# Layer 0's shift and scale summed by TensorE as columns, in a two-layer attention block on one core

## The chip, the core and the metric

The kernel runs on one core of a Trainium2 chip. The metric is the device time of one execution in microseconds (us). In the profile, PE is TensorE's matmuls, PEld its weight loads, DVE is VectorE, ACT is ScalarE, POOL is GpSimd and SP is SyncE, from whose queue the weights are loaded.

## The reference

Two layers, each with three kinds of attention in parallel (latent, windowed, axial), over 512 image tokens (x) and 256 context tokens (ctx) of width 1024. What matters here is how a layer begins: its input is normed, scaled and shifted by two vectors that are products of the conditioning rows with a 1024x3072 matrix.

```
def hybrid_layer(x, ctx, c, c_ctx, lw, pos, update_ctx):
    mod_x = jax.nn.silu(c) @ lw['ada_w'] + lw['ada_b']
    mod_c = jax.nn.silu(c_ctx) @ lw['ada_w'] + lw['ada_b']
    shift, scale, gate = jnp.split(mod_x[:, None, :], 3, axis=-1)
    c_shift, c_scale, c_gate = jnp.split(mod_c, 3, axis=-1)
    h = rmsnorm(x, lw['norm_w']) * (1 + scale) + shift
    hc = rmsnorm(ctx, lw['norm_w']) * (1 + c_scale) + c_shift
    p = h @ lw['w_in']
    ...
```

In layer 0 nothing can be projected before shift and scale are there.

## The kernel before

`schedule()` writes one list of events; `build()` then runs over that list once for each engine and issues what belongs to it, so the order of the list is the order on every engine. Tokens stand in six tiles of 128 (TT = 6): context tiles 0 and 1, image tiles 2 to 5. `first_modulation()` writes the start of layer 0, up to the first projections.

The first two thirds of `ada_w` (shift, then scale) are loaded as 16 chunks of 128 rows x 1024 columns, 512 KB each, into 16 buffers of their own (`FIRST`); D is 1024, KD is 8 and P is 128. The names w_raw_134 to w_raw_141 are the eight buffers of the shift third and w_raw_142 to w_raw_149 those of the scale third. `cs_n` holds silu of the two conditioning rows (x and ctx) as columns, 128x2 for each row chunk.

- The shift third is summed by VectorE. Event `AD` adds chunk times column for both rows of conditioning, into the PSUM tiles `wide` and `ptp`. Its last step writes into w_raw_140 and w_raw_141, and TensorE then sums over the partitions with `ones` as the moving operand, in a group of kind `adc` (lines 1394 and 2022).
- The scale third is summed by TensorE. Event `AF` (line 1414) holds `cs_n` (128x4, two columns of it zero) stationary and streams 512 columns of the chunk, twice per chunk. In the first five chunks a third matmul (line 1419) goes to `acc[1]`, where nobody reads it. ScalarE copies the two 4x512 sums to `a_row` (event `AC`, lines 1745 and 1746), and TensorE turns them into columns (event `AT`, line 1424).
- Event `MOD` (lines 2135 and 2141) adds the bias to the scale and forms `mod_a`; the shift is in `mod_col`.

A token tile goes through four events. `XQ`: ScalarE sums its squares and takes the root (lines 1789 and 1793). `XN`: the row is multiplied by its inverse root, into one of two buffers `xn`, by VectorE (line 2160) or by ScalarE (line 1801). `XT`: TensorE turns it, eight 128x128 transposes into `wide` or `ptp` (line 1497). `XM`: ScalarE and VectorE each scale and shift one half into one of two buffers `x_mod` (lines 1815 and 2180), ScalarE copies to `h_hi` (lines 1819 and 1822), GpSimd subtracts for `h_lo` (line 1912). Event `W` splits a weight chunk into `w_hi` (ScalarE, line 1632) and `w_lo` (GpSimd, line 1850). The projections' matmuls are at line 1394: w_raw_52 and w_raw_55 hold the two `early` chunks.

In the list, image tiles a and b (2 and 3) are normed and turned before `MOD`; c and d, and then the two context tiles, follow it. When context tile 1 is through, ScalarE squares the first projection (line 1648), VectorE reads it (lines 1969 and 1970), and TensorE goes on at 61.66 us with the next ones.

Of the kernel before, what the change touches and what calls it, by code (L numbers as in the profile page):

```python
# [5 lines left out]
D = 1024  # L6
# [3 lines left out]
P = 128  # L10
KD = D // P
# [115 lines left out]
def schedule():  # L127
# [414 lines left out]
    used, side_shift = {}, [0]  # L542

    def first_modulation():

        shift_row, shift_sums = row_sums(0, 0, FIRST[:KD])
        sums, scale = [], []
        for third in (0, 0, 0, 1, 0, 0, 1, 0, 1, 0, 1, 0, 1, 1, 1, 1):
            if third == 0:
                sums.append(shift_row(len(sums)))  # L550
            else:
                scale.append(chunk("adr", 0, 1, len(scale), (0, 1), slot=FIRST[KD + len(scale)]))
                whole.add(scale[-1])
                used[scale[-1]] = 0
        early = chunk("win", 0, C_AK, P), chunk("win", 0, C_CKV, P)
        a, b, c, d = x_first(0)[:4]
        holding[0] = True
        for k in range(KD):
            run_all(sums[k])
            emit("AF", c=scale[k], k=k)  # L560
            if k == 2:
                emit("VT")
            if k == KD - 3:
                emit("VC")
            if k == KD - 2:
                for tt in (a, b):
                    square_rows(0, tt, 0)
        for tt in (a, b):
            norm_rows(tt, by="v")
        emit("AC")  # L570
        run_all(shift_sums((0,)))
        turn_rows(a)
        emit("AT")
        turn_rows(b)
        emit("W", c=early[0])
        for tt in (c, d):
            square_rows(0, tt, 0)
        emit("W", c=early[1])
        n["split"] = early[1] + 1
        norm_rows(c)  # L580
# [11 lines left out]
        read_other()  # L592
        side_shift[0] = n["free"]
        for tt in x_first(0)[4:]:
            square_rows(0, tt, 0)
        norm_rows(x_first(0)[4])
        modulate_rows(d)
        holding[0] = False
# [30 lines left out]
    def norm_rows(tt, by="a"):  # L629
        emit("XN", tt=tt, n=row_of[tt], by=by)  # L630
# [4 lines left out]
    def modulate_rows(tt):  # L635
        emit("XM", tt=tt, n=row_of.pop(tt), mod=n["mod"], shift=side_shift[0] if tt < TT_CTX else 0)
# [285 lines left out]
def build(nc, t_in, out):  # L922
# [33 lines left out]
    cs_n = fixed("cs_n", [P, KD, 4], F)  # L956
# [46 lines left out]
    a_row = shared("a_row", [4, D], F, 83968)  # L1003
# [32 lines left out]
    with ExitStack() as stack:  # L1036
# [17 lines left out]
        af_done, at_done = semaphore("af_done"), semaphore("at_done")  # L1054
        row_copied = semaphore("row_copied")
# [106 lines left out]
        def _(sp):  # L1162
            new = counting()
            for c in range(len(chunks)):
# [74 lines left out]
        def first_sums(half):  # L1239
            return pv[0:4, :] if half == 0 else wide[0:4, D:D + 512]  # L1240
# [87 lines left out]
        def _(pe):  # L1328
# [5 lines left out]
            for e in events:  # L1334
# [72 lines left out]
                elif ev == "AF":  # L1407
                    c, k = e["c"], e["k"]
# [11 lines left out]
                elif ev == "AT":  # L1420
# [820 lines left out]
```

## Time and profile before

| | us |
|---|---|
| median of 3 runs | 1752.57 (1751.98 to 1753.06) |
| the profiled execution | 1752.6 |
| its span in the profile | 1750.8 |
| TensorE matmuls busy | 1673.6 (96%) |
| VectorE busy | 1022.5 (58%) |
| ScalarE busy | 1063.0 (61%) |
| GpSimd busy | 624.6 (36%) |
| mean granted TensorE clock | 0.991 of full |

Times in the trace count from the start of the span. A row of a timeline is one instruction or several alike in a row: its start, its length, what it is, how many records of it (x16), and in brackets how long the engine sat idle before it and for what. A float32 matmul that is no transpose leaves two records. PEclk is the clock that TensorE was granted, as a share of 2.4 GHz.

### The profile page before, as it was taken

The page shows a single profiled execution, that of the slowest core. Times are in us where ns is not written, and L with a number is a line of the kernel's source. Part 1 is how long each engine was busy: PE and PEld are TensorE (multiplying, and loading weights), DVE is VectorE, ACT ScalarE, POOL GpSimd, SP SyncE. Part 2 cuts the span into 40 slices and gives each one's busy share as a digit, 9 for nine tenths or more (in the row PEclk, how much of TensorE's full clock was granted, in tenths as well). Part 3 has the DMA queues.
Part 4 walks back from the last instruction along what each step waited for, and adds up shares of the span by engine and source line. Part 5 has one row for each costly group of instructions (what it writes and reads, how often), then busy time and mean ns, then how long its engine had stood idle before and what let it go on. Part 6 is the DMA issues. An engine that isn't in the chain of part 4 may idle for free.

```text
span 1750.8 us, 26994 instructions
## 1 busy us (share of the span) xinstructions
PE 1673.6 (96%) x10400; PEld 1465.8 (84%) x10400; DVE 1022.5 (58%) x2116; ACT 1063.0 (61%) x1967; POOL 624.6 (36%) x426
## 2 busy tenths in 40 slices
PE   6999999999999999999999999999999998999997
PEld 2778888889988889999889987888888887888787
DVE  6345766665556655545773535566676666555633
ACT  4545777776666767765321264678777678777322
POOL 1533333333333323322322254443344433333442
PEclk9999999999999999999999999999999999999999
DMA  8111111111111112011734322111122221212642
GB/s 321 52 37 29 26 46 37 49 31 49 49 55 49 33 41 55 25 44 47 234 115 171 119 76 73 41 38 46 49 55 67 73 73 33 70 51 53 204 146 95
DMA packets 178531, 129.51 MB, mean 74 GB/s; under 512 B 21658, under 2 KB 167652, under 8 KB 178404
## 3 DMA queue, kind: packets, MB, share of 16 engines
q1 hardware_dynamic: 174240, 115.36, 23.0%
q10 hardware_dynamic: 2884, 8.24, 1.3%
q0 software_dynamic: 1280, 4.20, 0.7%
q8 instruction: 82, 1.34, 0.3%
q14 instruction: 45, 0.37, 0.1%
HBM read 123.58 MB, written 4.19 MB: 73 GB/s over the span
## 4 chain that ended last, share of the span: by engine, by line
PE 74%; DVE 11%; ACT 10%; issue 3%; DMA 1%; POOL 0%; SPq 0%; DVEq 0%; ACTq 0%
PE acc L1394 54%; PE wide L1447 6%; PE ptp L1465 6%; PE pv L1478 4%; PE pv L1479 3%; DVE nmax L2067 2%; ACT e L1715 2%; DVE pt L2092 1%; ACT w_hi L1632 1%; DVE q_s L1584 1%; DVE k_m L1584 1%; DVE k_s L1584 1%; ACT k_m L1575 1%; ACT x_mod L1815 1%; DMA w_raw<-in_ada_w 1%
## 5 line engine op out<-in xcount | busy, mean ns | idle before, releaser
L1850 POOL TENSOR_TENSOR w_lo<-w_raw,w_hi 128x1024 fp32r<-128x1024 f32 (+2 forms) x192 | 391.0, 2039 | 562.8 <-ACT w_hi L1632 561.0
L1394 PE MATMUL acc<-h_hi,w_hi 128*128 128x512 f32 (+2 forms) x1320 | 464.7, 353 | 11.8 <-DVE lf L1970 4.7
L1394 PE MATMUL acc<-h_hi,w_lo 128*128 128x512 f32 (+2 forms) x1320 | 461.6, 351 | 0.0
L1394 PE MATMUL acc<-h_lo,w_hi 128*128 128x512 f32 (+2 forms) x1320 | 458.1, 351 | 0.6 <-POOL h_lo L1912 0.6
L1394 PEld LDWEIGHTS acc<-h_hi,w_hi 128*128 128x128 f32 (+1 forms) x1320 | 249.0, 189 | 50.5 <-issue 12.2
L1730 ACT ACTIVATE pt<-ptp 128x512 fp32r<-128x512 f32 (+3 forms) x312 | 165.5, 563 | 194.6 <-PE ptp L1465 192.7
L1394 PEld LDWEIGHTS acc<-h_hi,w_lo 128*128 128x128 f32 (+1 forms) x1320 | 248.9, 189 | 34.0
L1394 PEld LDWEIGHTS acc<-h_lo,w_hi 128*128 128x128 f32 (+1 forms) x1320 | 246.1, 188 | 34.9 <-POOL h_lo L1912 1.0
L2067 DVE TENSOR_REDUCE nmax<-wide 128x1 f32<-128x768 f32 (+3 forms) x240 | 190.1, 792 | 107.7 <-PE wide L1447 104.4
L1904 POOL TENSOR_TENSOR o_t<-o_half,o_t 64x256 f32<-64x256 f32 x120 | 91.4, 762 | 434.5 <-DVE o_half L2099 432.3
L1722 ACT ACTIVATE e<-e,einv 128x768 f32<-128x768 f32 (+3 forms) x240 | 193.4, 806 | 60.2 <-DVE einv L2084 59.7
L2092 DVE TENSOR_TENSOR pt<-ptp,pt 128x512 fp32r<-128x512 f32 (+3 forms) x312 | 192.0, 641 | 45.9 <-ACT pt L1730 45.8
L1632 ACT ACTIVATE w_hi<-w_raw 128x1024 fp32r<-128x1024 f32 (+2 forms) x192 | 172.8, 903 | 57.1 <-DMA w_raw<-in_w_out 53.9
L1465 PE MATMUL ptp<-ident,e 128*128 128x128 f32 x1152 | 161.4, 273 | 0.6 <-ACT e L1722 0.5
L1715 ACT ACTIVATE e<-wide,nbias,rq 128x768 f32<-128x768 f32 x160 | 144.9, 906 | 19.6 <-DVE nbias L2073 16.3
L1465 PEld LDWEIGHTS ptp<-ident,e 128*128 128x128 f32 x1152 | 131.1, 140 | 3.2 <-ACT e L1722 0.9
L1447 PE MATMUL wide<-k_s,q_s 128*128 128x256 f32 (+2 forms) x576 | 124.8, 334 | 0.0
L1478 PE MATMUL pv<-pt,v_s 128*128 128x256 f32 (+1 forms) x384 | 99.1, 285 | 13.2 <-DVE pt L2092 10.3
L1394 PE MATMUL acc<-og_hi,w_hi 128*128 128x512 f32 (+1 forms) x288 | 102.9, 357 | 0.0
L1394 PE MATMUL acc<-og_lo,w_hi 128*128 128x512 f32 (+1 forms) x288 | 102.7, 357 | 0.0
L1394 PE MATMUL acc<-og_hi,w_lo 128*128 128x512 f32 (+1 forms) x288 | 102.6, 356 | 0.0
L1479 PE MATMUL pv<-pt,v_s 128*128 128x256 f32 (+1 forms) x384 | 97.6, 282 | 0.0
(217 smaller groups left out, 3064.3 us busy)
## 6 DMA issues: line engine op xcount, KB each, us to landing
w_raw<-in_w_in SPq DMA_DIRECT2D x102, 512.0 KB, 3.9
w_raw<-in_ada_w SPq DMA_DIRECT2D x48, 512.0 KB, 5.5
w_raw<-in_w_out SPq DMA_DIRECT2D x16, 512.0 KB, 3.5
w_raw<-in_w_in SPq DMA_DIRECT2D x16, 256.0 KB, 3.1
w_raw<-in_w_o_mla SPq DMA_DIRECT2D x16, 256.0 KB, 2.8
w_raw<-in_w_o_swa SPq DMA_DIRECT2D x16, 256.0 KB, 2.8
w_raw<-in_w_o_ax SPq DMA_DIRECT2D x16, 256.0 KB, 2.8
w_raw<-in_mla_w_uq SPq DMA_DIRECT2D x16, 144.0 KB, 2.4
```

What stands on the lines that cost most here:

```text
L1394: ins = nc.tensor.matmul(dst, lhs, rhs, start=first, stop=last)
L1447: ins = nc.tensor.matmul(wide[:, c0:c0 + nk], lhs, rhs, start=(i == 0), stop=(i == len(pairs) - 1))
L1465: ins = nc.tensor.transpose(ptp_of(t)[:, b:b + P], e_of(u, c0, c0 + P), ident[:, :])
L1478: nc.tensor.matmul(dst, v_of(pa, kt), pt_of(t, 0)[:, b], start=t["first"] and i == 0, stop=False)
L1479: ins = nc.tensor.matmul(dst, v_of(pa, kt), pt_of(t, 1)[:, b], start=False, stop=t["last"] and i == len(t["blocks"]) - 1)
L1632: nc.scalar.activation(w_hi[s][:, 0:k], w_raw[s][:, 0:k], ACT.Copy).then_inc(w_hi_ready, 1)
L1715: nc.scalar.activation(e_of(u), wide[:, u["lo"]:u["lo"] + u["width"]], ACT.Exp, bias=nbias[:, r:r + 1], scale=scale, accum_out=esum[:, r:r ...
L1722: nc.scalar.activation(e_of(u), e_of(u), ACT.Copy, scale=einv[:, r:r + 1]).then_inc(norm_act, 1)
L1730: nc.scalar.activation(pt_of(t, 0), ptp_of(t), ACT.Copy).then_inc(pt_hi_ready, 1)
L1850: nc.gpsimd.tensor_tensor(w_lo[s][:, 0:k], w_raw[s][:, 0:k], f(w_hi[s][:, 0:k]), ALU.subtract).then_inc(w_lo_ready, 1)
L2067: link(nc.vector.tensor_reduce(nmax[:, r:r + 1], wide[:, u["lo"]:u["lo"] + u["width"]], AX.X, ALU.max, negate=True))
L2092: nc.vector.tensor_tensor(pt_of(t, 1), ptp_of(t), f(pt_of(t, 0)), ALU.subtract).then_inc(pt_lo_ready, 1)
```

## The change

All 16 chunks are summed by TensorE, and in the other form: each 128x128 block of a chunk is the stationary operand and the 128x2 column of `cs_n` streams past it. Eight such matmuls per chunk (line 1405 of the changed kernel) add into 16 columns of `pv`, so the sums come out as columns. VectorE sums nothing of it; the `adc` groups, `AC`, `AT`, `a_row` and the extra matmuls into `acc[1]` are gone. One matmul of the identity with zeros opens the accumulation. `MOD` waits for the last of these matmuls (`af_done`) and adds both biases. The two loads of x stand earlier in SP's queue, between the chunks. The transposes of a and b stand behind the 13th chunk, c and d are squared before `MOD`, and all six tiles of layer 0 are scaled by VectorE.

```diff
     def first_modulation():
...
+        for i in range(2 * KD):
+            emit("AF", c=rows[i], i=i)
+            if i == KD:
                 emit("VT")
...
+            if i == KD + 1:
                 emit("VC")
                 for tt in (a, b):
                     square_rows(0, tt, 0)
...
+                for tt in (a, b):
+                    norm_rows(tt)
+            if i == 2 * KD - 4:
+                turn_rows(a)
+                turn_rows(b)
+                for tt in (c, d):
+                    square_rows(0, tt, 0)
         emit("W", c=early[0])
...
         emit("MOD", l=0, free=n["free"])
         n["mod"] += 1
         modulate_rows(a)
-        norm_rows(d)
-        other_side, read_other = shift_sums((1,), defer=True)
-        run_all(other_side)
+        norm_rows(c)
         turn_rows(c)
         modulate_rows(b)
+        emit("W", c=early[1])
+        n["split"] = early[1] + 1
+        norm_rows(d)
+        turn_rows(d)
         load_table("s")
-        turn_rows(d)
         modulate_rows(c)
...
-                    for half in range(2):
-                        ins = nc.tensor.matmul(first_sums(half), cs_n[:, k, :], w_raw[slot_of[c]][:, half * 512:(half + 1) * 512],
-                                               start=(k == 0), stop=(k == KD - 1))
-                    if k == KD - 1:
+                    if i == 0:
+                        nc.tensor.matmul(pv[:, 0:4 * KD], ident[:, :], rot[:, 0:4 * KD], start=True, stop=False)
+                    for j in range(KD):
+                        at = 2 * (i // KD * KD + j)
+                        ins = nc.tensor.matmul(pv[:, at:at + 2], w_raw[slot_of[c]][:, j * P:(j + 1) * P], cs_n[:, i % KD, :],
+                                               start=False, stop=(i == 2 * KD - 1 and j == KD - 1))
+                    if i == 2 * KD - 1:
                         ins.then_inc(af_done, 1)
-                    if k < KD // 2 + 1:
-                        nc.tensor.matmul(acc[1][0:4, :], cs_n[:, k, :], w_raw[slot_of[c]][:, 0:512], start=True, stop=True)
...
-                if chunks[c][:4] == ("adr", 0, 1, KD // 2 + 1):
+                if chunks[c][:4] == ("adr", 0, 0, KD // 2):
                     sp.dma_start(xres[:, TT_CTX:TT_CTX + 2, :], x_rows[:, 0:2, :]).then_inc(x_load, 16)
-                if chunks[c][:3] == ("win", 0, C_AK):
+                if chunks[c][:4] == ("adr", 0, 1, 1):
                     sp.dma_start(xres[:, TT_CTX + 2:TT, :], x_rows[:, 2:, :]).then_inc(x_rest_load, 16)
...
-                        if new(at_done, 1):
-                            dve.wait_ge(at_done, 1)
-                        bias = vec[:, V_B0 + KD:V_B0 + 2 * KD].unsqueeze(2).to_broadcast([P, KD, 2])
-                        turned = pv[:, 0:4 * KD].rearrange("p (b s) -> p b s", s=4)
-                        link(nc.vector.tensor_tensor(turned[:, :, 0:2], turned[:, :, 0:2], bias, ALU.add))
+                        if new(af_done, 1):
+                            dve.wait_ge(af_done, 1)
+                        shift_b, scale_b = (vec[:, V_B0 + a * KD:V_B0 + (a + 1) * KD].unsqueeze(2).to_broadcast([P, KD, 2]) for a in range(2))
+                        turned = first_sums(1)
+                        nc.vector.tensor_tensor(mod_col[:, 0:KD, :], first_sums(0), shift_b, ALU.add)
+                        link(nc.vector.tensor_tensor(turned, turned, scale_b, ALU.add))
```

What it moves on TensorE, from the last chunks to the transposes of c and d. A row gives the line, the operation, out<-moving operand, stationary operand, the size of the output, a count, and the semaphores it waits for. Before:

```order
L1414 MATMUL pv<-w_raw_149,cs_n 4x512 [waits raw_load27]
L1414 MATMUL wide<-w_raw_149,cs_n 4x512
L1394 MATMUL acc<-ones,w_raw_140 128x2 [waits ada_used]
L1394 MATMUL acc<-ones,w_raw_140 128x2 x7
L1497 MATMUL wide<-ident,xn 128x128 [waits x_n]
L1497 MATMUL wide<-ident,xn 128x128 x7
L1424 MATMUL pv<-ident,a_row 128x4 [waits row_copied]
L1424 MATMUL pv<-ident,a_row 128x4 x7
L1497 MATMUL ptp<-ident,xn 128x128 [waits x_n]
L1497 MATMUL ptp<-ident,xn 128x128 x7
L1394 MATMUL acc<-ones,w_raw_141 128x2 x8
L1497 MATMUL wide<-ident,xn 128x128 [waits x_f,x_b,x_n]
```

In the changed kernel, from the 13th chunk on:

```order
L1405 MATMUL pv<-cs_n,w_raw_146 128x2 [waits raw_load24]
L1405 MATMUL pv<-cs_n,w_raw_146 128x2 x7
L1480 MATMUL wide<-ident,xn 128x128 [waits x_n]
L1480 MATMUL wide<-ident,xn 128x128 x7
L1480 MATMUL ptp<-ident,xn 128x128 [waits x_n]
L1480 MATMUL ptp<-ident,xn 128x128 x7
L1405 MATMUL pv<-cs_n,w_raw_147 128x2 [waits raw_load25]
L1405 MATMUL pv<-cs_n,w_raw_147 128x2 x7
L1405 MATMUL pv<-cs_n,w_raw_148 128x2 [waits raw_load26]
L1405 MATMUL pv<-cs_n,w_raw_148 128x2 x7
L1405 MATMUL pv<-cs_n,w_raw_149 128x2 [waits raw_load27]
L1405 MATMUL pv<-cs_n,w_raw_149 128x2 x7
```

Ahead of these stand twelve chunks in the same form, eight 128x2 matmuls each, with the transpose of `v_rows` between the ninth and the tenth. The transposes of a and b now stand ahead of the last three chunks, and nothing but `MOD` follows the last one before the transposes of c.

On ScalarE, around `MOD`, before:

```order
L1745 ACTIVATE a_row<-pv 4x512 [waits af_done,vec_ready]
L1746 ACTIVATE a_row<-wide 4x512
L1632 ACTIVATE w_hi_51<-w_raw_52 128x1024 [waits raw_load0]
L1789 ACTIVATE h_lo,ssq<-xres 128x8x128 [waits x_rest_load]
L1793 ACTIVATE rstd<-ssq,eps_col 128x1 [waits x_sq]
L1789 ACTIVATE h_lo,ssq<-xres 128x8x128
L1793 ACTIVATE rstd<-ssq,eps_col 128x1 [waits x_sq]
L1632 ACTIVATE w_hi_54<-w_raw_55 128x1024 [waits raw_load1]
L1801 ACTIVATE xn<-xres,rstd 128x1024 [waits x_t,x_inv]
L1815 ACTIVATE x_mod<-wide,mod_col,mod_a 128x128 [waits mod_ready]
L1815 ACTIVATE x_mod<-wide,mod_col,mod_a 128x128 x3
L1819 ACTIVATE h_hi<-x_mod 128x4x128 [waits x_b]
```

In the changed kernel:

```order
L1765 ACTIVATE h_lo,ssq<-xres 128x8x128 [waits x_rest_load]
L1769 ACTIVATE rstd<-ssq,eps_col 128x1 [waits x_sq]
L1765 ACTIVATE h_lo,ssq<-xres 128x8x128
L1769 ACTIVATE rstd<-ssq,eps_col 128x1 [waits x_sq]
L1615 ACTIVATE w_hi_51<-w_raw_52 128x1024 [waits raw_load0]
L1791 ACTIVATE x_mod<-wide,mod_col,mod_a 128x128 [waits mod_ready,x_t]
L1791 ACTIVATE x_mod<-wide,mod_col,mod_a 128x128 x3
L1795 ACTIVATE h_hi<-x_mod 128x4x128 [waits x_b]
L1798 ACTIVATE h_hi<-x_mod 128x4x128 [waits x_f]
L1791 ACTIVATE x_mod<-ptp,mod_col,mod_a 128x128 [waits x_t]
L1791 ACTIVATE x_mod<-ptp,mod_col,mod_a 128x128 x3
L1795 ACTIVATE h_hi<-x_mod 128x4x128 [waits x_b]
```

The two copies to `a_row` are gone, the split of the second early chunk (w_hi_54) stands behind tiles a and b, and none of the four `xn` scalings of line 1801 that stood behind `MOD` is left on ScalarE.

## Rows read from the trace of the kernel before

**Rows 1.** The page: shares, and the first lines of the slices
```profile
PE 1673.6 (96%) x10400; PEld 1465.8 (84%) x10400; DVE 1022.5 (58%) x2116; ACT 1063.0 (61%) x1967; POOL 624.6 (36%) x426
PE 74%; DVE 11%; ACT 10%; issue 3%; DMA 1%; POOL 0%; SPq 0%; DVEq 0%; ACTq 0%
```

**Rows 2.** The chain that ended last, window 0 to 90: start, us, what
```profile
3.74 10.61 DMA w_raw<-in_ada_w
...
14.39 1.02 PE pv L1414 x2
...
29.60 0.87 PE wide L1414 x2
...
30.57 0.59 ACT a_row L1745
...
61.66 16.00 PE acc L1394 x96
```

**Rows 3.** Timeline of TensorE, window 0 to 75
```profile
32.20 1.07 PE L1497 MATMUL wide<-ident,xn 128*128 128x128 f32 x8
...
42.29 1.94 PE L1497 MATMUL ptp<-ident,xn 128*128 128x128 f32 x8 [1.66 <-ACT x_mod L1815]
43.88 0.56 PE L1394 MATMUL acc<-h_hi,w_hi 128*128 128x256 f32 x1
```

**Rows 4.** Timeline of VectorE, window 0 to 75
```profile
7.75 1.29 DVE L2116 TENSOR_SCALAR wide<-w_raw,cs_n 128x1024 f32<-128x1024 f32 x1
...
34.05 0.16 DVE L2135 TENSOR_TENSOR pv<-pv,vec 128x16 f32<-128x16 f32 x1
...
34.60 1.37 DVE L2180 TENSOR_SCALAR x_mod<-wide,mod_a,mod_col 128x128 f32<-128x128 f32 x4
```

**Rows 5.** Timelines of TensorE, windows 924 to 926.4 and 926.46 to 929.2
```profile
924.07 2.48 PE L1394 MATMUL acc<-ones,w_raw 128*128 128x2 f32 x21 [0.18 <-DVE y L2015]
...
926.30 2.58 PE L1394 MATMUL acc<-ones,w_raw 128*128 128x2 f32 x12
928.74 0.77 PE L1394 MATMUL acc<-h_hi,w_hi 128*128 128x512 f32 x1
```

**Rows 6.** Timeline of TensorE, window 990 to 1008
```profile
998.04 3.63 PE L1394 MATMUL acc<-ones,w_raw 128*128 128x2 f32 x32
1001.53 0.56 PE L1394 MATMUL acc<-w_hi,y_hi 128*128 128x256 f32 x1
```

**Rows 7.** Stretches: length, busy PE, PEld, DVE, ACT, POOL, PEclk, DMA share, GB/s
```profile
14.40:30.30 15.90, 15.90 (x37) 2.96 (x37) 15.12 (x19) 4.06 (x7) 0.00 (x0) 1.00 1.04 409
924.10:926.40 2.30, 2.30 (x21) 2.30 (x22) 0.68 (x2) 1.75 (x3) 0.79 (x1) 1.00 0.56 187
926.50:928.70 2.20, 2.20 (x12) 2.20 (x12) 0.00 (x0) 0.00 (x0) 1.46 (x1) 0.50 0.08 28
998.10:1001.40 3.30, 3.30 (x32) 3.30 (x32) 0.86 (x2) 2.22 (x3) 0.00 (x0) 1.00 0.84 222
1001.60:1003.00 1.40, 1.40 (x8) 1.40 (x8) 0.48 (x4) 1.16 (x3) 0.00 (x0) 0.50 0.00 0
```

**Rows 8.** Timelines of ScalarE and GpSimd, window 0 to 75
```profile
35.22 1.04 ACT L1632 ACTIVATE w_hi<-w_raw 128x1024 fp32r<-128x1024 f32 x1
36.16 1.13 ACT L1801 ACTIVATE xn<-xres,rstd 128x1024 f32<-128x1024 f32 x1
37.20 1.48 ACT L1815 ACTIVATE x_mod<-wide,mod_col,mod_a 128x128 f32<-128x128 f32 x4
...
39.09 0.63 ACT L1822 ACTIVATE h_hi<-x_mod 128x512 fp32r<-128x512 f32 x1
...
45.47 1.09 ACT L1789 ACTIVATE h_lo<-xres 128x1024 fp32r<-128x1024 f32 x1
...
59.46 0.63 ACT L1648 ACTIVATE ak_sq<-acc 128x512 f32<-128x512 f32 x1
...
39.79 2.35 POOL L1912 TENSOR_TENSOR h_lo<-x_mod,h_hi 128x1024 fp32r<-128x1024 f32 x1 [1.12 <-ACT h_hi L1822]
```

More of the change, by code:

```diff
@@ L540, in load_rows @@
         return run
-    used, side_shift = {}, [0]
+    used = {}
     def first_modulation():
[L546 to L555, printed above, removed]
+        rows = []
+        for i in range(2 * KD):
+            if i == 2 * KD - 3:
+                early = [chunk("win", 0, C_AK, P)]
+            rows.append(chunk("adr", 0, i // KD, i % KD, (0, 1), slot=FIRST[i]))
+            whole.add(rows[-1])
+            used[rows[-1]] = 0
+        early.append(chunk("win", 0, C_CKV, P))
         a, b, c, d = x_first(0)[:4]
         holding[0] = True
[L558 to L561, printed above, removed]
+        for i in range(2 * KD):
+            emit("AF", c=rows[i], i=i)
+            if i == KD:
                 emit("VT")
-            if k == KD - 3:
+            if i == KD + 1:
                 emit("VC")
-            if k == KD - 2:
                 for tt in (a, b):
                     square_rows(0, tt, 0)
[L568 to L574, printed above, removed]
-        emit("W", c=early[0])
[L576 to L580, printed above, removed]
+                for tt in (a, b):
[5 more added lines that the diff above has]
+                    square_rows(0, tt, 0)
+        emit("W", c=early[0])
         emit("MOD", l=0, free=n["free"])
@@ L627, in square_rows, with norm_rows @@
         n["x"] += 1
-    def norm_rows(tt, by="a"):
-        emit("XN", tt=tt, n=row_of[tt], by=by)
+    def norm_rows(tt):
+        emit("XN", tt=tt, n=row_of[tt], by="v" if row_of[tt] < TT else "a")
     def turn_rows(tt):
@@ L635, in modulate_rows @@
     def modulate_rows(tt):
-        emit("XM", tt=tt, n=row_of.pop(tt), mod=n["mod"], shift=side_shift[0] if tt < TT_CTX else 0)
+        emit("XM", tt=tt, n=row_of.pop(tt), mod=n["mod"])
     def next_norm(l, added):
@@ L955, in build @@
     vec, vec_sw = fixed("vec", [P, V_ROWS], F), fixed("vec_sw", [P, V_ROWS], F)
-    cs_n = fixed("cs_n", [P, KD, 4], F)
+    cs_n = fixed("cs_n", [P, KD, 2], F)
     cs_f = fixed("cs_f", [P, 2, 2 * KD], F)
@@ L1237, in xt_of, with first_sums @@
             return wide[:, 0:D] if i % 2 == 0 else ptp[:, 0:D]
-        def first_sums(half):
-            return pv[0:4, :] if half == 0 else wide[0:4, D:D + 512]
+        def first_sums(third):
+            return pv[:, 2 * KD * third:2 * KD * (third + 1)].rearrange("p (j s) -> p j s", s=2)
         def o_tokens(pa):
@@ L1412, in _ @@
                         pe.wait_ge(raw_load[slot_of[c]], loads[c])
-                    for half in range(2):
-                        ins = nc.tensor.matmul(first_sums(half), cs_n[:, k, :], w_raw[slot_of[c]][:, half * 512:(half + 1) * 512],
-                                               start=(k == 0), stop=(k == KD - 1))
-                    if k == KD - 1:
-                        ins.then_inc(af_done, 1)
-                    if k < KD // 2 + 1:
-                        nc.tensor.matmul(acc[1][0:4, :], cs_n[:, k, :], w_raw[slot_of[c]][:, 0:512], start=True, stop=True)
-                elif ev == "AT":
-                    if new(row_copied, 1):
-                        pe.wait_ge(row_copied, 1)
-                    for j in range(KD):
-                        ins = nc.tensor.transpose(pv[:, 4 * j:4 * j + 4], a_row[0:4, j * P:(j + 1) * P], ident[0:4, 0:4])
-                    ins.then_inc(at_done, 1)
+                    if i == 0:
[5 more added lines that the diff above has]
+                    if i == 2 * KD - 1:
+                        ins.then_inc(af_done, 1)
                 elif ev in ("SA", "SB"):
@@ L1939, in _ @@
             silu = cs_f[:, 0, :].rearrange("p (s k) -> p k s", s=2)
-            link(nc.vector.memset(cs_n[:, :, 2:4], 0.0))
-            nc.vector.tensor_copy(cs_n[:, :, 0:2], silu).then_inc(cs_ready, 1)
+            link(nc.vector.memset(rot[:, 0:4 * KD], 0.0))
+            nc.vector.tensor_copy(cs_n[:, :, :], silu).then_inc(cs_ready, 1)
             for e in events:
@@ L2017, in _ @@
                         cols_ = slice(g["third"] * KD, (g["third"] + 1) * KD)
-                        b0 = V_B + (g["l"] - 1) * 2 * KD if g["l"] else V_B0
+                        b0 = V_B + (g["l"] - 1) * 2 * KD
                         s0, s1 = g["only"][0], g["only"][-1] + 1
@@ L2157, in _ @@
                         if e["by"] == "v":
+                            if i >= 2:
+                                if new(x_t, i - 1):
+                                    dve.wait_ge(x_t, i - 1)
                             if new(x_inv, i + 1):
@@ L2172, in _ @@
                         dve.wait_ge(mod_ready, e["mod"])
-                    if new(acc_free, e["shift"]):
-                        dve.wait_ge(acc_free, e["shift"])
                     if i >= 2:
```

19 lines of the change are left out of this document (4 added, 15 removed).

## The prediction

> **What bounds the kernel now.** First the page: TensorE is busy for 96% of the span and holds 74% of the chain that ended last [rows 1]. Late work on TensorE is late for good, and what matters is when its unbroken run begins. Then the chain, in order of time: up to 61.66 us it is the start-up, and from 61.66 a run of 96 records begins [rows 2]. Nothing behind that point is changed in its order, so the change is worth the shift of the 61.66. The reader should see who holds the chain ahead of it: the loads of ada_w until 14.39, TensorE's sums of the scale third until 30.5, then ScalarE, from `a_row` at 30.57. The third view, VectorE's timeline, gives the two marks of the working: `cs_n` is ready and the first chunk is there at 7.75, and shift and scale are ready when the x_mod row starts, at 34.60 [rows 4]. Call this second mark T. From T to 61.66 it takes 27.06 us. So the question falls in two: where does T go, and how long is the way from T on.
>
> **T: the chunks on TensorE.** Before, a chunk of the scale third costs TensorE two matmuls of 512 columns, two records and 0.87 us each at full clock [rows 2], in eight chunks, and there are five extra matmuls of the same size. Now 16 chunks cost eight float32 matmuls each, which are 16 records of the form 128x2 with a fresh 128x128 stationary operand. That is 256 records. The trace has this very form with `ones` moving, as part of layer 1, and it has it at both clocks:
> - at full clock 32 records begin at 998.04 and the next matmul starts at 1001.53, which is 0.109 us each [rows 6];
> - at PEclk 0.50, 12 records begin at 926.30 and the next matmul starts at 928.74, which is 0.203 each [rows 5, 7]. The first of them began at full clock; without it the other eleven are 0.212 each. I take 0.21.
>
> So the sums cost 256 x 0.109 = 27.9 us at 2.4 GHz, or 256 x 0.21 = 53.8 us at 1.2 GHz. The clock decides the case.
>
> **The clock.** Before, the first chunks moved 512 columns for each load of weights, and the clock stood at 1.00 from 14.40 to 30.30, with the weight loads busy for only 2.96 of 15.90 us [rows 7]. The new stream is the opposite: two columns for each load. Two places show what the chip makes of it. From 998.1 to 1001.4 TensorE is busy without a gap with nothing but this form, PEclk 1.00, and right behind it, at 1001.6, the clock is 0.50 [rows 6, 7]. From 924.1 the same happens: 21 records at 1.00, then the rest at 0.50, with TensorE busy in every microsecond [rows 5, 7]. In neither place does an idle gap explain the fall; 0.18 us is all that stands ahead of the second. So a stream of loads with two columns each lost the clock twice, each time from full clock. In the changed kernel nothing with many columns runs ahead of it or beside it for 13 chunks. I take it that the clock never rises there.
>
> The Trainium skill, "TensorE: Matmul & The Clock Gate", the section on why this matters for your kernels, tells one to keep TensorE busy without long idle gaps, and its full clock follows. By that rule the stream, which has no gap, would run at 2.4 GHz and the sum would be that of the first rival below. The rows at 998.1 to 1003.0 disagree: busy all the time, and the clock fell. The same page, section "LDWEIGHTS (loading the stationary operand)", gives 128 columns a load of 107 ns whatever the clock, which again would be the first rival; at PEclk 0.50 the measured 0.203 to 0.212 is twice that.
>
> T then, step by step:
> - start 7.8 [rows 4]; the loads are no bound, since the last chunk is the 21st half megabyte in the queue, 11.0 MB at 409 GB/s [rows 7] is 27 us, while TensorE comes to it near 62;
> - the identity times zeros, 2 records at low clock, estimated as two of the 0.21: 0.4;
> - 256 records, 53.8;
> - the transpose of v_rows, estimated as two of them too, 0.4;
> - the transposes of a and b, 16: at low clock eight take from 42.29 to 43.88, 1.6 [rows 3], so 3.2. They are ready long before (x is loaded and squared early, VectorE has nothing else to do), but they now stand in line ahead of three chunks;
> - drain 0.2, and MOD: from 34.05 to 34.60 it took 0.55 [rows 4], with one more addition of 0.16, 0.7.
>
> Sum 7.8 + 0.4 + 53.8 + 0.4 + 3.2 + 0.9 = 66.5, against 34.60.
>
> What goes at no cost: VectorE's sums, ScalarE's a_row, the `adc` groups. They hid behind each other and nothing of them would be on the path at T = 66.5.
>
> **From T on.** Before, ScalarE began the first tile only at 37.20, 2.6 us after T, because squares, a weight split and an `xn` scaling stood ahead [rows 4, 8]. Now it waits with nothing ahead: 2.6 saved. From 37.20 to the square of the first projection at 59.46 it was busy nearly without a break, and there, too, three more `xn` scalings went by, of about 1.04 each (36.16 to 37.20) [rows 8]: 3.1 saved, and 1.0 comes back with the second early split (1.04 at 35.22). VectorE takes these scalings in its idle time: between 34.60 and 61.66 ScalarE is the one that the chain runs over. That is 27.06 - 2.6 - 3.1 + 1.0 = 22.4. GpSimd has three tiles' h_lo and one more split of 2.35 each behind T [rows 8] and stays inside that. TensorE is at low clock behind T, now as before (eight transposes 1.94 against 1.07 at 32.20 [rows 3]), and context tile 1 can only be turned behind the second half of the first projection; I add 0.7. So 23.1 us, between 22.4 and, if the waits between the engines eat all savings, 27.1.
>
> TensorE's run begins at 66.5 + 23.1 = 89.6, against 61.66: 28.0 us later. The profiled execution took 1752.6, its span 1750.8, the median 1752.57; the sum is made against 1752.6. Forecast: 1752.6 + 28.0 = 1780.6 us, slower by 1.6%.
>
> **The rivals.**
> - *The clock is full for the stream* (7%). For it: the skill's rule. Against: both places of rows 7. Allow 1.6 us for a slow beginning: T = 7.8 + 0.2 + 27.9 + 1.6 + 0.2 + 1.8 + 0.9 = 40.4, and with 23.1 the run begins at 63.5, 1.8 us late: 1754.4, within 0.2% (3.5 us, about what a measurement of this kernel can tell from no change).
> - *The other side: the way from T shrinks by more than T grows* (1%). It needs the full clock as well, T = 40.4, and less than 17.8 us from T on to be 3.5 us faster. ScalarE's own work on six tiles, 2.4 each from 37.20 to 39.6 [rows 8], with squares and splits, is already near 20. With 20 it would be 1751.3.
> - *The clock comes back on the way* (27%). The 16 transposes in a row are denser in columns. For it: eight transposes took 1.07 at 32.20, among work of few columns, and the clock was full [rows 3]. Against: eight at 42.29 ran at the low clock from end to end, and what follows the new ones is the stream that loses the clock. At most the last three chunks run at full clock: 48 x (0.21 - 0.109) = 4.8 saved, 1775.8. If the rise comes earlier and is lost again several times, down to 1770.
> - *The way from T stays 27.1* (10%): 1784.6, because GpSimd's queue, with a split and two table loads between tiles b and c, holds up the buffers x_mod.
> - *Low clock throughout, as summed* (55%): 1780.6.
>
> **How the numbers follow.** With 0.203 a record the sum falls by 1.8, with 0.215 it rises by 1.3; the way from T may be 22.4 to 27.1. That and the partial return of the clock give 1774 to 1786, which leaves out the first two rivals and the deep end of the third. Slower by over 0.2%: 0.92. Within: 0.07. Faster: 0.01.
>
> **What would show it.** The timeline of TensorE from 7.8 on should be 16 blocks of records 128x2, about 3.4 us each, PEclk 0.50 until about 65; the weight loads busy all through; x_mod's first row at 66 to 67, and the long run of the projections at 89 to 90. Right about the clock but not about the way: x_mod at 66.5 and the run elsewhere. Wrong: blocks of 1.75 us. Behind the run's start the old trace should reappear, shifted as a whole. The prediction falls if PEclk reads 1.00 between 10 and 60.

## The result, and the profile after

The changed kernel takes 1785.95 us (median of 4 runs, 1783.06 to 1789.11) against 1752.55 (1751.98 to 1753.06): a ratio of 1.0191, 95% interval 1.0179 to 1.0204, or 33.4 us slower. The forecast was 1780.6. The profiled execution took 1789.11 us with a span of 1787.3, the slowest of the four; its repeat (below) had a span of 1780.7.

First the page of the changed kernel, with the shares and the chain that ended last:

```profile
PE 1705.8 (95%) x10576; PEld 1515.3 (85%) x10576; DVE 1014.3 (57%) x2103; ACT 1058.1 (59%) x1961; POOL 625.6 (35%) x426
PE 74%; DVE 12%; ACT 10%; issue 3%; DMA 1%; POOL 0%; ACTq 0%; DVEq 0%; SPq 0%
```

The shares are nearly those of [rows 1]. They can't show a loss of 2%; the marks T and the start of the run must. TensorE's timeline of the changed kernel:

```profile
8.30 0.63 PE L1402 MATMUL pv<-rot,ident 128*128 128x32 f32 x2 [1.45 <-DVE cs_n L1917]
8.75 30.86 PE L1405 MATMUL pv<-cs_n,w_raw 128*128 128x2 f32 x144
39.47 0.37 PE L1394 MATMUL acc<-ident,v_rows 78*128 78x78 f32 x1
39.63 13.73 PE L1405 MATMUL pv<-cs_n,w_raw 128*128 128x2 f32 x64
53.23 1.95 PE L1480 MATMUL wide<-ident,xn 128*128 128x128 f32 x8
54.97 1.92 PE L1480 MATMUL ptp<-ident,xn 128*128 128x128 f32 x8
56.67 10.24 PE L1405 MATMUL pv<-cs_n,w_raw 128*128 128x2 f32 x48
...
89.05 1.26 PE L1480 MATMUL ptp<-ident,xn 128*128 128x128 f32 x8 [3.87 <-DVE xn L2140]
...
96.73 0.76 PE L1382 MATMUL acc<-h_hi,w_hi 128*128 128x512 f32 x1 [2.21 <-DVE lf L1946]
```

The 256 records take 54.6 us: from 8.75 to 39.47 there are 144, which is 0.213 each, and 0.213 again in the 64 and in the 48. Eight transposes take 1.95, as at the low clock in [rows 3]. TensorE's run begins at 96.73, where before it was 61.66 [rows 2]: 35.07 us later, of 36.5 by which the span grew. The other 1.4 lie behind that point and were not followed; they are no loss of the change, for that part of the span differs between executions by more (below).

T is where x_mod's first row starts. VectorE's, ScalarE's and GpSimd's timelines of the changed kernel:

```profile
67.60 1.36 DVE L2158 TENSOR_SCALAR x_mod<-wide,mod_a,mod_col 128x128 f32<-128x128 f32 x4
...
69.07 0.75 DVE L2140 TENSOR_SCALAR xn<-xres,rstd 128x1024 f32<-128x1024 f32 x1
...
71.20 1.97 DVE L2140 TENSOR_SCALAR xn<-xres,rstd 128x1024 f32<-128x1024 f32 x1
...
77.35 0.16 DVE L2133 RECIPROCAL rstd<-rstd 128x1 f32<-128x1 f32 x1 [2.90 <-ACT rstd L1769]
77.54 0.79 DVE L2140 TENSOR_SCALAR xn<-xres,rstd 128x1024 f32<-128x1024 f32 x1
78.25 1.35 DVE L2158 TENSOR_SCALAR x_mod<-ptp,mod_a,mod_col 128x128 f32<-128x128 f32 x4
...
82.39 6.61 DVE L2140 TENSOR_SCALAR xn<-xres,rstd 128x1024 f32<-128x1024 f32 x1
...
89.71 1.35 DVE L2158 TENSOR_SCALAR x_mod<-wide,mod_a,mod_col 128x128 f32<-128x128 f32 x4
...
79.64 0.63 ACT L1795 ACTIVATE h_hi<-x_mod 128x512 fp32r<-128x512 f32 x1 [0.94 <-DVE x_mod L2158]
...
91.10 0.63 ACT L1795 ACTIVATE h_hi<-x_mod 128x512 fp32r<-128x512 f32 x1 [5.66 <-DVE x_mod L2158]
...
70.22 5.20 POOL L1888 TENSOR_TENSOR h_lo<-x_mod,h_hi 128x1024 fp32r<-128x1024 f32 x2 [36.52 <-ACT h_hi L1798]
75.39 2.39 POOL L1826 TENSOR_TENSOR w_lo<-w_raw,w_hi 128x1024 fp32r<-128x1024 f32 x1
...
79.01 4.81 POOL L1888 TENSOR_TENSOR h_lo<-x_mod,h_hi 128x1024 fp32r<-128x1024 f32 x2
83.78 4.66 POOL L1826 TENSOR_TENSOR w_lo<-w_raw,w_hi 128x1024 fp32r<-128x1024 f32 x2
```

T is 67.60, so the way from T to the run takes 29.1 us. The four xn rows are the four later scalings (image tiles c and d, context tiles 0 and 1). One instruction has two prices: 0.75 for c, 6.61 for context tile 1. The long one begins 3.38 us after the start of GpSimd's unbroken row of four (two h_lo, two w_lo, 79.01 to 88.44) and ends at 89.00, half a microsecond behind the row's end. VectorE's half of x_mod for context tile 0 stands behind it and starts at 89.71, and ScalarE waits 5.66 us for that. ScalarE waits once more, 0.94 us, for x_mod of image tile d (78.25). No long scaling causes this one: x_mod of d stands in VectorE's queue behind the scaling of context tile 0 (0.79), and that scaling had to wait for ScalarE's own root of this tile (2.90, until 77.35).

The stretches of the changed kernel have the columns of [rows 7]:

```profile
9.00:20.00 11.00, 11.00 (x53) 11.00 (x54) 0.00 (x0) 4.48 (x8) 0.00 (x0) 1.00 0.99 384
```

Here stands a trap. The clock's column prints 1.00 where 53 records fill 11.00 us, twice the price of [rows 6]. The experiments show which of the two is to be believed.

### The profile page after: what moved, and what is told of

It reads as the page before. It is cut to its first block, busy times and chain, and to the rows that moved or that the text cites. A ratio compares the mean times of both kernels' runs of the same rounds, so it can differ in the third digit from the quotient of the medians.

```text
span 1787.3 us, 27316 instructions
## 1 busy us (share of the span) xinstructions
PE 1705.8 (95%) x10576; PEld 1515.3 (85%) x10576; DVE 1014.3 (57%) x2103; ACT 1058.1 (59%) x1961; POOL 625.6 (35%) x426
## 4 chain that ended last, share of the span: by engine, by line
PE 74%; DVE 12%; ACT 10%; issue 3%; DMA 1%; POOL 0%; ACTq 0%; DVEq 0%; SPq 0%
PE acc L1382 52%; PE wide L1430 6%; PE ptp L1448 5%; PE pv L1461 4%; PE pv L1462 3%; PE pv L1405 3%; DVE nmax L2043 2%; ACT e L1698 2%; DVE pt L2068 1%; ACT w_hi L1615 1%; DVE q_s L1567 1%; DVE k_m L1567 1%; DVE k_s L1567 1%; ACT k_m L1558 1%; ACT x_mod L1791 1%
```

## The experiments

The kernel before, timed beside each of them on the same chip, took 1752.5 to 1752.7. T and the run's start are from each one's own profiled execution. From the run's start to the end of the span these executions took 1682.9 to 1691.6 us, though nothing in that part was changed. So the two marks tell more of the start-up than a difference of two or three us between medians.

| | median us (range) | ratio (95%) | T | run starts | T to run |
|---|---|---|---|---|---|
| changed kernel | 1785.95 (1783.06 to 1789.11) | 1.0191 (1.0179 to 1.0204) | 67.60 | 96.73 | 29.1 |
| its repeat | 1783.30 (1781.34 to 1784.70) | 1.0175 (1.0161 to 1.0189) | 64.14 | 93.25 | 29.1 |
| all four scalings on ScalarE | 1779.52 (1776.09 to 1785.42) | 1.0154 (1.0137 to 1.0172) | 64.23 | 91.39 | 27.2 |
| context tile 1 on ScalarE | 1779.16 (1779.03 to 1781.77) | 1.0149 (1.0135 to 1.0163) | 64.16 | 88.90 | 24.7 |
| 128 columns | 1760.89 (1755.78 to 1766.25) | 1.0043 (1.0027 to 1.0059) | 42.09 | 71.19 | 29.1 |
| 128 columns, four on ScalarE | 1759.51 (1758.80 to 1759.83) | 1.0036 (1.0024 to 1.0048) | 41.71 | 69.30 | 27.6 |
| 128 columns, context tile 1 on ScalarE | 1755.81 (1754.70 to 1757.16) | 1.0014 (1.0005 to 1.0023) | 41.58 | 66.31 | 24.7 |
| scaling with a sum | 1789.13 (1787.80 to 1792.41) | 1.0215 (1.0201 to 1.0229) | 67.26 | 95.75 | 28.5 |
| before, four on VectorE | 1751.23 (1749.74 to 1753.97) | 0.9989 (0.9980 to 0.9997) | 36.46 | 60.80 | 24.3 |
| before, d and context tile 1 on VectorE | 1751.40 (1749.42 to 1753.54) | 0.9990 (0.9981 to 0.9999) | 34.55 | 60.24 | 25.7 |
| before, no extra matmuls | 1752.90 (1750.83 to 1754.53) | 0.9998 (0.9989 to 1.0007) | 34.83 | 61.92 | 27.1 |
| before, scale third as columns | 1754.16 (1752.04 to 1755.50) | 1.0007 (0.9998 to 1.0015) | 35.22 | 62.30 | 27.1 |
| the same, d and context tile 1 on VectorE | 1752.53 (1750.77 to 1754.54) | 1.0001 (0.9992 to 1.0010) | 35.75 | 61.46 | 25.7 |

### What the clock costs: 128 columns instead of two

The moving operand is widened by 126 columns of zeros, which change no sum; the opening matmul and its zeros are widened with it. Number and size of the weight loads stay.

```diff
+    cs_w = nc.alloc_sbuf_tensor_at("cs_w", [P, KD, 128], F, offset=cos_at)
...
-                        ins = nc.tensor.matmul(pv[:, at:at + 2], w_raw[slot_of[c]][:, j * P:(j + 1) * P], cs_n[:, i % KD, :],
+                        ins = nc.tensor.matmul(pv[:, at:at + 128], w_raw[slot_of[c]][:, j * P:(j + 1) * P], cs_w[:, i % KD, :],
```

> The changed kernel, but the moving operand of each of the 128 sum matmuls has 128 columns instead of 2: the two of silu and 126 of zeros, which add nothing to the neighbouring sums in PSUM. Weight loads, their number and their order are the same. Theory (columns): the low clock came from the few columns moved per load; with 128 the clock rises within the first chunks, a record stays at 0.11 us at full clock because the load still sets the pace, the 256 records take 28 to 31 us, shift and scale are ready at 41 to 45, and the time is 1758 to 1763 (with the 6.6 us on VectorE still in). Rival (the start of the program is slow whatever is moved, or the pace is the load's and does not depend on the clock): records at 0.21 us, shift and scale at 67 or later, 1786 or more.

TensorE's timeline with 128 columns:

```profile
8.58 18.47 PE L1407 MATMUL pv<-cs_w,w_raw 128*128 128x128 f32 x144
...
26.95 7.35 PE L1407 MATMUL pv<-cs_w,w_raw 128*128 128x128 f32 x64
34.14 1.04 PE L1482 MATMUL wide<-ident,xn 128*128 128x128 f32 x8
```

and its stretches:

```profile
9.00:13.00 4.00, 4.00 (x20) 4.00 (x20) 0.00 (x0) 0.42 (x1) 0.00 (x0) 1.00 0.92 319
...
14.00:26.00 12.00, 12.00 (x110) 12.00 (x110) 0.00 (x0) 5.44 (x11) 0.00 (x0) 1.00 1.03 412
```

Up to 13 us a record takes 0.2 (20 in 4.00 us), from 14 on about 0.11 (110 in 12.00; 0.112 in the row of 64, from 26.95 to 34.14), with 64 times the columns. The weight loads are the same and busy without a gap in both kernels. So the load's own time follows the clock, and here it was the added columns that brought the clock up. T falls by 25.5 us against the first trace and 22.1 against the repeat, and the time by 25.1 (22.4). The clock is the cause of most of the loss. The way from T doesn't change: 29.1 again, with a scaling of 6.58.

The changed kernel once more, unchanged, shows the other side of the same thing.

> The changed kernel itself once more, for the spread between its executions and a second profile. In its first profile all 256 records ran at 0.21 us and the run began at 96.7; in two variants the 16 transposes between the chunks were followed by about 3.4 us at full clock and shift and scale came at 64.2 instead of 67.6. If that is chance in each execution: times spread over 1781 to 1789 with a median near 1785, and this profile has shift and scale at either 64.2 or 67.6 and 29.1 us from there to the run in both cases. If the first profile was an odd one: all times within 1 us of each other.

Its timeline of TensorE at the transposes of a and b:

```profile
52.89 1.95 PE L1480 MATMUL wide<-ident,xn 128*128 128x128 f32 x8
54.63 1.50 PE L1480 MATMUL ptp<-ident,xn 128*128 128x128 f32 x8
55.97 7.49 PE L1405 MATMUL pv<-cs_n,w_raw 128*128 128x2 f32 x48
```

and two stretches of the stream right behind them:

```profile
56.00:59.40 3.40, 3.40 (x32) 3.40 (x30) 0.00 (x0) 0.00 (x0) 0.00 (x0) 0.94 0.00 0
59.50:63.50 4.00, 3.96 (x19) 3.87 (x19) 0.01 (x1) 0.00 (x0) 0.00 (x0) 0.50 0.00 0
```

This time the clock rose within the second eight transposes (1.50 instead of 1.92), then it fell to 0.50 in the middle of the stream, where 19 records take 4.0 us. (The 32 of the first stretch include records that only reach into it, the last transposes among them.) The stream of 48 took 7.49 instead of 10.24, which is what some 27 records at 0.112 instead of 0.213 save. That is the third place where this stream lost a full clock, after the two of [rows 7]. T is 64.14 instead of 67.60: 2.75 of it from the stream, 0.36 from the transposes and 0.34 from an earlier start. It also settles the trap: once the clock's record has changes in it, 0.50 stands beside 0.21 us a record. The same price in the first 50 us is the low clock, and the 1.00 printed there is no reading. So some 3.1 us of the spread between executions of the changed kernel are this.

### What lengthens the way: the scalings

```diff
-        emit("XN", tt=tt, n=row_of[tt], by="v" if row_of[tt] < TT else "a")
+        emit("XN", tt=tt, n=row_of[tt], by="v" if row_of[tt] < 2 else "a")
```

> The changed kernel, but image tiles c and d and both context tiles get their row scaling xn from ScalarE again, as before the change; a and b stay on VectorE. Theory (port): the scaling of context tile 1 took 6.61 us on VectorE because GpSimd's splits, 128x1024 back to back, held it off until they ended; on ScalarE the four cost 1.04 each and nothing waits 5.7 us for x_mod. ScalarE's row gets 4.2 longer and loses waits of about 6.6, so TensorE's long run starts 2 to 4 us earlier than 96.73, at 93 to 95, and the time falls from 1786 to about 1783. Rival (the wait was for something else, an order of semaphores or the load of x): the delay stays between the square of context tile 1 and its transpose, and ScalarE's 4.2 us come on top, 1790. Shift and scale ready unchanged at 67 to 68 in both.

The way falls by 1.9 only, from 29.1 to 27.2, since ScalarE, over which the chain runs, now carries four scalings of 1.13 to 1.16. With `< 5` in place of `< 2` just context tile 1 goes back to ScalarE:

> The changed kernel with one scaling moved: context tile 1's xn is made by ScalarE (1.1 us) instead of VectorE (6.61 us in the changed kernel). c, d and context tile 0 stay on VectorE. Theory (VectorE held off by GpSimd's back-to-back splits; the 6.0 us that the way from shift and scale to TensorE's run came out too long are this one instruction): from x_mod's first row to the run 23.5 to 25 us instead of 29.1, and about 4.5 us less than the changed kernel's time if shift and scale come at 67.6, 1781 (1777 where the clock is full for three chunks). Rival (ScalarE is the limit wherever the scaling stands): 27, as with all four on ScalarE.

VectorE's, ScalarE's and GpSimd's timelines of that kernel:

```profile
65.63 0.75 DVE L2140 TENSOR_SCALAR xn<-xres,rstd 128x1024 f32<-128x1024 f32 x1
...
67.77 1.94 DVE L2140 TENSOR_SCALAR xn<-xres,rstd 128x1024 f32<-128x1024 f32 x1
...
74.12 0.75 DVE L2140 TENSOR_SCALAR xn<-xres,rstd 128x1024 f32<-128x1024 f32 x1
...
78.81 1.80 DVE L2124 TENSOR_SCALAR cos<-cos,vec 128x512 f32<-128x512 f32 x1
...
78.93 1.15 ACT L1777 ACTIVATE xn<-xres,rstd 128x1024 f32<-128x1024 f32 x1 [0.23 <-DVE rstd L2133]
...
81.11 4.74 POOL L1826 TENSOR_TENSOR w_lo<-w_raw,w_hi 128x1024 fp32r<-128x1024 f32 x2 [0.79 <-ACT w_hi L1615]
```

The way is 24.7, 4.4 shorter, for 1.15 us of work on the busier engine. Part of this is a second effect of the same edit. The next instruction on VectorE, the scaling of `cos`, was held as well (1.80, where 0.47 is its free time), but only until GpSimd's h_lo ended: ScalarE's split of the weights now comes later, and GpSimd stood idle for 0.79 us before its two w_lo. The edit opened a gap in GpSimd's row. The median is no better than with all four on ScalarE (1779.16 against 1779.52), though the way is 2.5 shorter; the difference lies behind the run's start, which says that these two medians can't rank them. Both edits on top of the 128 columns, first all four, then context tile 1:

> Both edits together: 128 columns per sum matmul (126 of them zeros) and the row scalings of c, d and the context tiles on ScalarE. If the low clock and VectorE's wait are all that the change lost: shift and scale ready at 41 to 45, from there 26 us to TensorE's run, so the run starts at 67 to 71 against 61.66 before, and the time is 1757 to 1762. If something else in the change costs time as well, it stays above 1765.

> 128 moving columns (126 of them zeros) and context tile 1's scaling on ScalarE. If the clock and this one scaling are all that was lost: shift and scale at 42, run at 66 to 67 against 61.66 before, 1756 to 1758, still 4 to 5 us slower than before. The rest is then TensorE's load-bound sum, 256 records at 0.11 us each, against 8 chunks on TensorE and 8 on VectorE side by side.

27.6 and 24.7: the two causes add up without touching each other. The best column form is still 0.14% behind the kernel before (1.0014, 1.0005 to 1.0023).

Why is the scaling held? The last run keeps it on VectorE in its place, but in the form that also writes the sum of the row, which nobody reads.

```diff
+                            if i == 5:
+                                nc.vector.tensor_scalar(xn[:, i % 2, :], xres[:, tt, :], rstd[:, tt:tt + 1], 0.0, ALU.mult, ALU.add, accum_out=xn_sum[:, :]).then_inc(x_n, 1)
```

> The changed kernel; VectorE still scales context tile 1 into xn at the same place, but by the form of the instruction that also writes the sum of the row (a number nobody reads). In the changed kernel this scaling took 6.60 and 6.61 us beside GpSimd's three operations in a row. Theory A, it is the fast form of the scaling (0.75 us for 1024 columns when GpSimd is idle) that cannot run while GpSimd holds something both need: the form with the sum takes one column per cycle, some 1.1 to 1.3 us, but it is not held up. Then the scaling takes 1.1 to 1.4 us at its place, the way from x_mod's first row to TensorE's run is 29.1 - 5.3 = about 24 us (23.5 to 25), and the time falls from 1783 to 1786 to 1778 to 1781, ratio 1.014 to 1.016. Theory B, VectorE is kept from any scaling of this size by GpSimd, or by a buffer or a signal that GpSimd owns: the scaling takes 6.6 us or more again, the way is 29 us or longer, and the time is that of the changed kernel, 1781 to 1786. The Trainium skill's page on SBUF says the first of the form with the sum, that it stays out of the modes that take the shared ports.

VectorE's and GpSimd's timelines of this kernel:

```profile
82.03 1.28 DVE L2142 TENSOR_SCALAR_CACHE_REDUCE xn<-xres,rstd 128x1024 f32<-128x1024 f32 x1
83.23 0.08 DVE L2142 DVE_READ_ACCUMULATOR xn<-xres,rstd 128x1 f32 x1
83.23 5.18 DVE L2125 TENSOR_SCALAR cos<-cos,vec 128x512 f32<-128x512 f32 x1
88.33 0.47 DVE L2126 TENSOR_SCALAR sin<-sin,vec_sw 128x512 f32<-128x512 f32 x1
...
78.64 4.77 POOL L1889 TENSOR_TENSOR h_lo<-x_mod,h_hi 128x1024 fp32r<-128x1024 f32 x2
83.37 4.75 POOL L1827 TENSOR_TENSOR w_lo<-w_raw,w_hi 128x1024 fp32r<-128x1024 f32 x2
```

The sum form ran in 1.28 us in the middle of GpSimd's row, so the instruction's part of theory A holds and B falls. Its time for the kernel was wrong: the next instruction on VectorE is the scaling of `cos` in the fast form, 0.47 us when free, and that one now stood for 5.18 us until GpSimd's row ended (88.12), with x_mod queued behind it. The way was 28.5, and the median, 1789.13, didn't fall at all (its trace has the late T, 67.26, and the longest part of all behind the run's start, 1691.6). What is held is the fast form from SBUF to SBUF, whichever stands next; x_mod's rows, which read PSUM, take their 1.36 beside GpSimd as without.

The Trainium skill, "SBUF — State Buffer", the section "Who interferes with whom", says that a VectorE instruction in a mode that uses two ports and any GpSimd instruction exclude each other for the whole instruction, and that `tensor_scalar` can enter such a mode, but not in the form that writes its accumulator. The 6.61, 1.28 and 5.18 agree. The sentence speaks of one instruction, 2.4 us here; the wait lasted over the rest of a row of four.

A row without a gap does not hold VectorE in every case. The scaling of d (71.20 to 73.17 in the changed kernel) met the pair at 70.22 and was let in between its two h_lo: the first took 2.39 and ended at 72.61, the second 2.77. The input of the second, `h_hi`, had been done for 0.04 us only when the first ended. In the row of four the inputs of the two w_lo had been done for 0.7 and 2.1 us when their turn came, and VectorE got in before neither. That this is the difference is read from these rows and was not tested.

### Parts of it applied to the kernel before

Four scalings on VectorE in the kernel before, by the change's own rule (`"v" if row_of[tt] < TT`, with a wait for the buffer's transposes):

> The kernel before, with one part of the change alone: VectorE scales the rows of tiles c, d and both context tiles (xn) instead of ScalarE. Theory (port): GpSimd has splits and h_lo back to back from 54.3 to 63.6 there, and single ones with gaps before; a scaling on VectorE that falls beside one waits for its end, 1 to 6 us each; against it stand the four scalings of 1.04 that ScalarE loses. TensorE's run at 61.66 moves by -3 to +4, with single scalings of well over 0.75 us in VectorE's timeline. Rival (VectorE and GpSimd do not disturb each other): each scaling takes 0.75, ScalarE's row shortens by 3 to 4, 1748.5 to 1750.

VectorE's scalings there:

```profile
34.74 1.32 DVE L2163 TENSOR_SCALAR xn<-xres,rstd 128x1024 f32<-128x1024 f32 x1
...
38.00 1.73 DVE L2163 TENSOR_SCALAR xn<-xres,rstd 128x1024 f32<-128x1024 f32 x1
...
46.22 2.61 DVE L2163 TENSOR_SCALAR xn<-xres,rstd 128x1024 f32<-128x1024 f32 x1
...
50.21 0.75 DVE L2163 TENSOR_SCALAR xn<-xres,rstd 128x1024 f32<-128x1024 f32 x1
```

Three of four are held, none for longer than 1.9 us, for GpSimd's instructions stand singly in this order. The first of them stands ahead of x_mod, and T slips from 34.60 to 36.46; the way shrinks by 2.7, and 0.9 remain. Next, only d and context tile 1 go to VectorE (`"v" if row_of[tt] in (0, 1, 3, 5)`); the one ahead of x_mod and the longest one, 2.61, stay on ScalarE.

> The kernel before with the scalings of image tile d and context tile 1 on VectorE; c and context tile 0 stay on ScalarE. With all four on VectorE c's (1.32 us) stood ahead of shift and scale and context tile 0's waited beside GpSimd (2.61 us, ScalarE idle 1.39). Theory (port): only those two cost, so the run starts 1.5 to 2.5 us before 61.66 and the time is 1750 to 1751. Rival: the same as with all four, 1751.2, or no gain, 1752.5.

It gave as much as all four on VectorE, and the further gain that was expected didn't come: T stays at 34.55, and the way is 25.7. Both are about 0.1% faster than the kernel before, with intervals that just leave out 1, and are the fastest versions here.

The extra matmuls into `acc[1]` are left out:

```diff
-                    if k < KD // 2 + 1:
-                        nc.tensor.matmul(acc[1][0:4, :], cs_n[:, k, :], w_raw[slot_of[c]][:, 0:512], start=True, stop=True)
```

> The kernel before without the five matmuls into acc[1] that nobody reads. Theory (columns): each takes 0.87 us of TensorE, but the sums of the scale then follow the chunks' landing with gaps; 512 columns per load keep the share of moved columns high, so the clock should hold in most executions; TensorE's sums end no earlier than the last chunk, near 30, and the time is 1750 to 1753. Rival (any gap or thinner work there costs the clock): the scale's chunks take 1.7 us per matmul pair at half clock, shift and scale come 2 to 6 us late, 1755 to 1759.

TensorE's timeline of it:

```profile
14.56 1.87 PE L1414 MATMUL pv<-w_raw,cs_n 128*4 128x512 f32 x2 [1.69 <-DMA w_raw<-in_ada_w]
...
17.88 1.02 PE L1414 MATMUL pv<-w_raw,cs_n 128*4 128x512 f32 x2
...
27.10 1.02 PE L1414 MATMUL pv<-w_raw,cs_n 128*4 128x512 f32 x2 [1.43 <-DMA w_raw<-in_ada_w]
```

The clock comes up at 17.9 instead of by 14.4 [rows 2, 7], but TensorE still waits for a late chunk (1.43 us at 27.10), and nothing is lost: the loads bound this part.

Then the scale third alone in column form with 128 columns, no `AC`, `AT` or extra matmuls, VectorE keeping the shift third:

```diff
+                    for j in range(KD):
+                        ins = nc.tensor.matmul(pv[:, 2 * j:2 * j + 128], w_raw[slot_of[c]][:, j * P:(j + 1) * P], cs_w[:, k, :],
```

> The kernel before with one part of the change alone, and without its two faults: the scale third is summed in columns (weights of the chunk stationary, 128 moving columns of which 126 are zeros), VectorE keeps the shift third, the copies to a_row, the transposes back and the extra matmuls are gone, and ScalarE keeps its row scalings. Eight chunks at about 1.75 us each (16 records of 0.11) are no more than TensorE spent on them before, and the last is bound by its landing near 29. Theory (the column form itself is sound, the clock and the sixteen chunks in one row made it slow): shift and scale at 32.5 to 34.6, ScalarE free of a_row (1.1 us) starts its first tile at 36 to 37, run at 60.3 to 61.5, 1751 to 1752.5. Rival (column sums cost more than rows at any clock): run at 62.5 or later, 1754 or more.

ScalarE's timeline, where `a_row` was:

```profile
30.48 1.06 ACT L1632 ACTIVATE w_hi<-w_raw 128x1024 fp32r<-128x1024 f32 x1 [0.60 <-DMA w_raw<-in_w_in]
33.08 1.07 ACT L1789 ACTIVATE h_lo<-xres 128x1024 fp32r<-128x1024 f32 x1 [1.54 <-DMA xres<-in_x]
```

The freed time is lost to the load of x, for which ScalarE waits 1.54 us. T is 35.22 and the time 1754.16. My expectation of a gain missed: it priced what ScalarE drops, and not what it would wait for next. With d and context tile 1 on VectorE as well:

> The same, and the row scalings of image tile d and context tile 1 on VectorE, as in the best split tried before. If the gains add: run at 58.8 to 60.2, 1749.5 to 1751, faster than both the kernel before and the changed one. If ScalarE is no longer what is waited for, the second gain is lost and it equals the one with the scale in columns alone.

No difference from before (1.0001).

## Why the prediction was right and wrong

**The bound, and what the change is worth.** Right. The run's start moved by 35.07 of the span's 36.5 us. That it is the only thing that moves the time was too strong: behind it the executions differ by up to 8.7 us among themselves.

**T.** Right in mechanism and nearly in size: 67.60 against 66.5. A record took 0.213 and not 0.21 (0.8 us over 256), and the stream began 0.5 later; the other terms together are 0.2 shorter. For the drain of 0.2 no row was given; in the trace 0.04 lie between the last record's end (66.91) and VectorE's start (66.95). The clock never rose during the first 208 records, as reasoned from [rows 5 to 7], and the 128 columns show that the two columns a load were why. The rule of keeping TensorE busy, from the Trainium skill, "TensorE: Matmul & The Clock Gate", the section on why this matters for your kernels, would have given 1754.4. The changed kernel and the one with 128 columns both kept it busy in every microsecond of the stretches shown, and the clocks differed. The repeat shows the third rival, the clock's return with the transposes, as half true: 3.1 us where at most 4.8 were named, in three of the five traces with two columns.

**The way from T.** Here the prediction failed. The step is "VectorE takes these scalings in its idle time", with which ScalarE's own row gave 22.4, only 0.7 was allowed on top of it, and the way was 23.1. The way was 29.1 in both traces of the changed kernel. ScalarE's own row was right: 29.1 less its two waits is 22.5, where 22.4 was summed. The waits were 6.6 (0.94 and 5.66), and this is the term that was wrong.

Two things were overlooked. The scalings had x_mod queued behind them on VectorE, for which ScalarE waits; this order alone makes the 0.94, and it is still there (0.90) with context tile 1 on ScalarE. And their price was taken from instructions beside an idle GpSimd. The kernel before has only such rows, and here are two of them, of VectorE and then GpSimd:

```profile
28.59 0.75 DVE L2160 TENSOR_SCALAR xn<-xres,rstd 128x1024 f32<-128x1024 f32 x1
...
32.65 2.37 POOL L1850 TENSOR_TENSOR w_lo<-w_raw,w_hi 128x1024 fp32r<-128x1024 f32 x1 [32.20 <-ACT w_hi L1632]
```

The new order puts the last scaling into GpSimd's longest row up to there, and this makes the 5.66. GpSimd's work was undercounted as well: the prediction gave it three h_lo and one split behind T and said that it "stays inside that", but up to 88.44 the trace has four h_lo and three w_lo there, and the same work is in the trace of the kernel before. With context tile 1 on ScalarE the way is 24.7: the 22.5, the scaling that ScalarE took back (1.06 to the next start, with 0.23 of waiting before it) and the 0.90. The 0.7 added for turning context tile 1 appears nowhere. So the waits were 5.9 longer than the 0.7 allowed, and the forecast was 5.4 too low.

**The bounds.** The 27.1 was no upper bound. It supposed that waits eat all savings, not that a new wait could be longer than they are. The upper end of the range, 1786, was made with it, and the median of 1785.95 stands at this end. The rival of the unshortened way (1784.6, 10%) came nearest and named GpSimd, but for another reason, the buffers x_mod; no row of the changed kernel shows a wait for those.

**The other side.** It needed the full clock and a way of 17.8 us. The full clock was made in three experiments, and the shortest way from T seen in any kernel was 24.3.

**The marks.** "PEclk 0.50 until about 65" and "the prediction falls if PEclk reads 1.00 between 10 and 60" were bad marks. The column prints 1.00 there, and the prediction doesn't fall, because the lengths of the records (0.213 against 0.109) tell the clock. The blocks of 3.4 us and T at 66 to 67 were good ones; the run was to start at 89 to 90 and the mark said at once that the way was off.

**What is left.** Medians put about 22 to 25 us on the clock (to 1760.9) and 5.1 on the scaling of context tile 1 (to 1755.8). The last 3.3 against the kernel before go with T, 41.6 against 34.6, which the shorter way (24.7 against 27.1) makes good in part. How the 5.1 divide between the scaling itself and the gap that its move opened in GpSimd's row was not measured.

## What to carry to other kernels

Here a stream of weight loads with two columns each left TensorE at half its clock for 50 us, though it was busy in every microsecond, and the loads cost double too (0.213 instead of 0.112); the busy share of 100% said nothing of the clock. An instruction moved to an idle engine is priced beside what its neighbours will be doing at that moment, and with what is queued behind it. VectorE's fast scaling from SBUF to SBUF beside GpSimd cost as much as the rest of GpSimd's unbroken row: place it in a gap, or keep it on ScalarE, and then look at the next fast instruction on VectorE, which inherits the wait. Read a clock from the lengths of known records before trusting a printed 1.00 at the start of a trace.

## What the runs showed of the hardware that was not expected

- A scaling of 0.75 us stood for 6.58 to 6.61 us in three traces, over the rest of an `h_lo` and two `w_lo` of GpSimd that followed without a gap and whose inputs had been done before. Between two `h_lo`, the second of which had just got its input, it was let in (1.97). In the sum form the same scaling took 1.28, and the hold passed to the next fast instruction, 5.18.
- Within 16 transposes of 128 columns each the clock rose in some executions (the second eight took 1.50, then a part of the stream ran at 0.112 a record) and not in others (1.92), with the same instructions ahead.
- 126 columns of zeros added to each matmul made the same 144 weight loads faster by 12 us (18.3 instead of 30.7).
